# Feed-forward gate and up products: the high and low inputs as one 512-column moving operand, the halves added at eviction, and one set of accumulator banks in place of two

## What is computed

```
def swiglu(h, w_in, w_out):
    a, b = jnp.split(h @ w_in, 2, axis=-1)
    return (jax.nn.silu(a) * b) @ w_out
```

## Time and profile before

| | |
|---|---|
| Time before, median of 3 runs | 2448.12 us (2444.57 to 2448.9) |
| The profiled execution's own time | 2446.43 us |
| Its span | 2444.6 us, 35444 instructions |
| PE busy | 2278.1 us (93%), 15482 matmuls |
| PEld busy | 2061.0 us (84%) |
| DVE busy | 1291.6 us (53%) |
| ACT busy | 873.9 us (36%) |
| DMA | 373.10 MB, mean 153 GB/s |
| Mean granted clock of PE | 0.961 |

### The profile page before, as it was taken

One profiled execution on the slowest core, in us unless ns is written; L12 is line 12 of the kernel. 1 busy time (PEld: TensorE's weight loads), 2 busy tenths in 40 slices (PEclk: granted clock), 3 DMA queues, 4 the chain that ended last, 5 costly groups with the idle time before them and its releaser, 6 DMA issues.

```text
span 2444.6 us, 35444 instructions
## 1 busy us (share of the span) xinstructions
PE 2278.1 (93%) x15482; PEld 2061.0 (84%) x15482; DVE 1291.6 (53%) x1485; ACT 873.9 (36%) x889; POOL 123.3 (5%) x68
## 2 busy tenths in 40 slices
PE   6999889999999898999999899997999998889997
PEld 4887779999999568998998789987999886879996
DVE  4458535555653355546546545554555767535554
ACT  3313324335332143333334433333333442124332
POOL 0157200000000000000000000000000110000000
PEclk8999999999999999999999989998999996999998
DMA  7329604554554204555554315552455340024551
GB/s 305 115 101 390 290 1 179 183 184 172 180 183 170 77 2 154 184 182 184 189 187 157 121 69 189 182 183 99 176 185 189 123 171 1 1 71 157 182 184 52
DMA packets 52481, 373.10 MB, mean 153 GB/s; under 512 B 5728, under 2 KB 6752, under 8 KB 7840
## 3 DMA queue, kind: packets, MB, share of 16 engines
q1 hardware_dynamic: 51584, 367.78, 41.3%
q0 software_dynamic: 800, 3.93, 0.4%
HBM read 370.64 MB, written 1.05 MB: 152 GB/s over the span
## 4 chain that ended last, share of the span: by engine, by line
PE 89%; DVE 6%; ACT 3%; DMA 1%; issue 1%; POOL 0%; SPq 0%; DVEq 0%; ACTq 0%; POOLq 0%
PE PS L354 11%; PE PS L353 11%; PE PS L352 11%; PE PS L368 5%; PE PS L369 5%; PE PS L370 5%; PE PS L308 5%; PE PS L601 3%; PE PS L1267 2%; PE PS L753 2%; PE PS L290 2%; PE PS L291 2%; PE PS L192 2%; PE PS L292 2%; PE PS L273 2%; PE PS L274 2%
## 5 line engine op out<-in xcount | busy, mean ns | idle before, releaser
L473 DVE TENSOR_TENSOR ring_r<-ring,AR_r 128x2048 fp32r<-128x2048 f32 x274 | 628.3, 2298 | 584.9 <-ACT AR_r L467 584.9
L467 ACT ACTIVATE AR_r<-ring 128x2048 fp32r<-128x2048 f32 x274 | 522.2, 1911 | 584.2 <-PE PS L370 237.8
L352 PE MATMUL PS<-AR_r 128*128 128x256 f32 x2240 | 634.1, 283 | 0.0
L354 PE MATMUL PS<-AR_r,ring_r 128*128 128x256 f32 x2240 | 633.9, 283 | 0.0
L353 PE MATMUL PS<-AR_r 128*128 128x256 f32 x2240 | 633.9, 283 | 0.0
L353 PEld LDWEIGHTS PS<-AR_r 128*128 128x128 f32 x2240 | 429.8, 192 | 2.5
L352 PEld LDWEIGHTS PS<-AR_r 128*128 128x128 f32 x2240 | 429.8, 192 | 2.5
L354 PEld LDWEIGHTS PS<-AR_r,ring_r 128*128 128x128 f32 x2240 | 429.7, 192 | 0.0
L368 PE MATMUL PS<-AR_r 128*128 128x512 f32 x616 | 240.7, 391 | 0.0
L369 PE MATMUL PS<-ring_r,AR_r 128*128 128x512 f32 x616 | 240.5, 390 | 0.0
L370 PE MATMUL PS<-AR_r 128*128 128x512 f32 x616 | 239.6, 389 | 0.0
(11 more groups left out here) (362 smaller groups left out, 3146.8 us busy)
## 6 DMA issues: line engine op xcount, KB each, us to landing
ring<-stream SPq DMA_DIRECT2D x346, 1024.0 KB, 4.8
X<-xt SPq DMA_DIRECT2D x1, 2048.0 KB, 9.5
AR<-bias POOLq DMA_DIRECT2D x1, 1536.0 KB, 8.3
AR<-pt POOLq DMA_DIRECT2D x2, 512.0 KB, 4.2
out<-X SPq DMA_DIRECT2D x1, 1024.0 KB, 4.8
SM<-small SPq DMA_DIRECT2D x1, 545.0 KB, 4.0
AR<-invc SPq DMA_DIRECT2D x1, 512.0 KB, 15.1
X<-negl POOLq DMA_DIRECT2D x1, 512.0 KB, 7.5
```

The source lines that it names most:

```text
L352: pe.matmul(o, w_hi, X_HI[:, k, :], start=(k == 0), stop=False)
L354: ins = pe.matmul(o, w_lo, X_HI[:, k, :], start=False, stop=(k == DT - 1))
L467: act.activation(w_hi_of(tag, i), ring[:, n % SLOTS, :], ACT.Identity).then_inc(split_hi, 1)
L473: dve.tensor_tensor(RING_R[:, n % SLOTS, :], ring[:, n % SLOTS, :], w_hi_of(tag, i), ALU.subtract).then_inc(split_lo, 1)
```

## The change

`X_PARTS` is a view of the same memory as `X_HI` and `X_LO` with the two as its halves: for each `k` it gives 2 runs of 256 columns, 4096 elements apart. In `gate_up` one matmul of 512 columns with `w_hi` takes the place of the two of 256, and writes a whole bank: `w_hi*X_HI` into columns 0 to 255, `w_hi*X_LO` into columns 256 to 511. The matmul with `w_lo` adds to columns 0 to 255 as before. So each output tile `j` takes a bank of its own: the gate has banks 6 and 7 and the up product banks 4 and 5, in every step, where before steps went to two sets in turn. Step 0 is left as it was, in banks 4 and 5.

The two halves are added on the way out: ACT copies the low halves of both banks of the gate into `GATE` and of the up product into `HIDDEN` (`low_part`), DVE adds the high halves from the banks (new lines in `step` and `gating`), and silu and the products then work in place, outside the banks. A new semaphore `ffn_low` counts ACT's copies and `ffn_gate_taken` DVE's additions of the gate. PE waits for `ffn_gate_taken` of the step before ahead of a gate chunk, and for `ffn_gated` of the step before ahead of an up chunk.

```
@@ -141,6 +141,8 @@
         multiplied = S["chunk_multiplied"]
         ffn_silu = S["ffn_silu"]
         ffn_hidden = S["ffn_hidden"]
+        ffn_low = S["ffn_low"]
+        ffn_gate_taken = S["ffn_gate_taken"]
         ffn_gated = S["ffn_gated"]
         split_hi = S["split_hi"]
         split_lo = S["split_lo"]
@@ -172,6 +174,7 @@
         TURN_OF = {"ffn1_lat": 2, "ffn2": 2, "mix2_in": 2}
         w_hi_of = lambda tag, i: W0_HI[i % 3] if tag == "mix0_in" else W_HI[(i + TURN_OF.get(tag, 0)) % 3]
         X_HI, X_LO = (arena(at, DT, T, of=AR_R) for at in (12288, 16384))
+        X_PARTS = AR_R[:, 12288:20480].rearrange("p (s n) -> p s n", s=2)
         G_HI, G_LO = (arena(18432 + 1024 * i, 2, 2, T, of=AR_R) for i in range(2))
 
         def need_chunk(eng, n):
@@ -339,19 +342,22 @@
 
                 pe.wait_ge(split_lo, r + (s0 + i + 1))
 
-            def gate_up(d, i, r):
+            def gate_up(i, step, steps, r):
 
                 for half in range(2):
                     n = n0 + i + half
                     need_split(r, i + half)
+                    if half:
+                        pe.wait_ge(ffn_gated, steps + (g0 + step))
+                    elif c or step > 1:
+                        pe.wait_ge(ffn_gate_taken, steps + (c * (FF_STEPS - 1) + step - 1))
                     for j in range(2):
-                        o = PS[:, 4 + 2 * d + half, j * T:(j + 1) * T]
+                        bank = (6, 4)[half] + j
                         for k in range(DT):
                             w = slice(k * 256 + j * P, k * 256 + (j + 1) * P)
                             w_hi, w_lo = w_hi_of(tag, i + half)[:, w], RING_R[:, n % SLOTS, w]
-                            pe.matmul(o, w_hi, X_HI[:, k, :], start=(k == 0), stop=False)
-                            pe.matmul(o, w_hi, X_LO[:, k, :], start=False, stop=False)
-                            ins = pe.matmul(o, w_lo, X_HI[:, k, :], start=False, stop=(k == DT - 1))
+                            pe.matmul(PS[:, bank, :], w_hi, X_PARTS[:, :, k * T:(k + 1) * T], start=(k == 0), stop=False, skip_group_check=True)
+                            ins = pe.matmul(PS[:, bank, 0:T], w_lo, X_HI[:, k, :], start=False, stop=(k == DT - 1), skip_group_check=True)
                     ins.then_inc(multiplied, 1)
 
             def down(d, i, last, r):
@@ -384,12 +390,12 @@
             first = 0
             if sums:
                 turn()
-                gate_up(1, 2, 0)
+                gate_up(2, 1, 0, 0)
                 sums()
                 open_sums()
                 pe.wait_ge(ffn_gated, g0 + 1)
                 down(0, 4, False, 0)
-                gate_up(0, 5, 0)
+                gate_up(5, 2, 0, 0)
                 pe.wait_ge(ffn_gated, g0 + 2)
                 down(1, 7, False, 0)
                 first = 2
@@ -398,7 +404,7 @@
             with pe.Fori(0, (FF_STEPS - 1 - first) // 2) as r:
                 for it in (first + 1, first + 2):
 
-                    gate_up(it % 2, 3 * it - 1, r * 6)
+                    gate_up(3 * it - 1, it, r * 2, r * 6)
 
                     pe.wait_ge(ffn_gated, r * 2 + (g0 + it))
                     down((it - 1) % 2, 3 * it + 1, False, r * 6)
@@ -497,29 +503,46 @@
         def act_ffn(act, order, tag, between=None):
             n0 = START[tag]
 
-            def silu(it, r=0):
-
-                act.wait_ge(multiplied, r + (n0 + max(3 * it - 1, 0) + 1))
-                act.activation(GATE[:, it % 2, :], PS[:, 4 + 2 * (it % 2), :], ACT.Silu).then_inc(ffn_silu, 1)
-
-            def splits(it, r=0, turns=0):
-
-                for i in range(3 * it + (2 if it else 3), min(3 * it + 5, FF_CHUNKS)):
-                    act_split_chunk(act, tag, i, r, turns)
+            def silu(it, steps=0):
+
+                if it == 0:
+                    act.wait_ge(multiplied, n0 + 1)
+                    act.activation(GATE[:, 0, :], PS[:, 4, :], ACT.Silu).then_inc(ffn_silu, 1)
+                else:
+                    act.wait_ge(ffn_gate_taken, steps + (FFN_INDEX[tag] * (FF_STEPS - 1) + it))
+                    act.activation(GATE[:, it % 2, :], GATE[:, it % 2, :], ACT.Silu).then_inc(ffn_silu, 1)
+
+            def low_part(it, up, steps=0, r=0):
+                act.wait_ge(multiplied, r + (n0 + 3 * it + up))
+                if it >= 2:
+                    act.wait_ge(ffn_gated, steps + (FFN_INDEX[tag] * FF_STEPS + it - 1))
+                out, bank = (HIDDEN, 4) if up else (GATE, 6)
+                act.activation(out[:, it % 2, :].rearrange("p (j t) -> p j t", j=2), PS[:, bank:bank + 2, T:T2], ACT.Identity).then_inc(ffn_low, 1)
+
+            def splits(chunks, r=0, turns=0):
+
+                for i in chunks:
+                    if i < FF_CHUNKS:
+                        act_split_chunk(act, tag, i, r, turns)
+
+            def step(it, steps=0, r=0, turns=0):
+                low_part(it, 0, steps, r)
+                splits((3 * it + 2,), r, turns)
+                silu(it, steps)
+                low_part(it, 1, steps, r)
+                splits((3 * it + 3, 3 * it + 4), r, turns)
 
             act_table(act, order, ACT.Silu)
             silu(0)
-            splits(0)
+            splits((3, 4))
             if between:
                 between()
                 act_table(act, order, ACT.Silu)
             with act.Fori(0, (FF_STEPS - 3) // 2) as r:
                 for it in (1, 2):
-                    silu(it, r * 6)
-                    splits(it, r * 6, r)
+                    step(it, r * 2, r * 6, r)
             for it in (FF_STEPS - 2, FF_STEPS - 1):
-                silu(it)
-                splits(it)
+                step(it)
             act_ln_exp(act)
 
 
@@ -529,16 +552,22 @@
 
             def gating(it, steps=0, r=0):
                 d = it % 2
-                dve.wait_ge(ffn_silu, steps + (g0 + it + 1))
-
-                dve.wait_ge(multiplied, r + (n0 + (3 * it if it else 1) + 1))
+                gate, up = GATE[:, d, :], HIDDEN[:, d, :]
+                if it:
+                    dve.wait_ge(ffn_low, steps * 2 + (2 * FFN_INDEX[tag] * (FF_STEPS - 1) + 2 * it))
+                    halves_up = up.rearrange("p (j t) -> p j t", j=2)
+                    dve.tensor_tensor(halves_up, halves_up, PS[:, 4:6, 0:T], ALU.add).then_inc(ffn_hidden, 1)
+                else:
+                    dve.wait_ge(multiplied, n0 + 2)
+                    dve.tensor_copy(up, PS[:, 5, :]).then_inc(ffn_hidden, 1)
                 if it >= 2:
                     dve.wait_ge(multiplied, r + (n0 + 3 * it - 1))
-                gate, up = GATE[:, d, :], PS[:, 5 + 2 * d, :]
+                dve.wait_ge(ffn_silu, steps + (g0 + it + 1))
+                dve.wait_ge(ffn_hidden, steps * 3 + (3 * (g0 + it) + 1))
                 both = lambda ap: ap[:, d, :, :].rearrange("p a b -> p (a b)")
                 dve.tensor_tensor(both(G_HI), gate, up, ALU.mult).then_inc(ffn_hidden, 1)
-                dve.tensor_tensor(HIDDEN[:, d, :], gate, up, ALU.mult).then_inc(ffn_hidden, 1)
-                dve.wait_ge(ffn_hidden, steps * 2 + 2 * (g0 + it + 1))
+                dve.tensor_tensor(up, gate, up, ALU.mult).then_inc(ffn_hidden, 1)
+                dve.wait_ge(ffn_hidden, steps * 3 + 3 * (g0 + it + 1))
                 dve.tensor_tensor(both(G_LO), HIDDEN[:, d, :], both(G_HI), ALU.subtract).then_inc(ffn_gated, 1)
 
             gating(0)
@@ -548,6 +577,9 @@
                 add()
 
             def step(it, steps=0, r=0):
+                gate = GATE[:, it % 2, :].rearrange("p (j t) -> p j t", j=2)
+                dve.wait_ge(ffn_low, steps * 2 + (2 * FFN_INDEX[tag] * (FF_STEPS - 1) + 2 * it - 1))
+                dve.tensor_tensor(gate, gate, PS[:, 6:8, 0:T], ALU.add).then_inc(ffn_gate_taken, 1)
                 dve_split_chunk(dve, tag, 3 * it + 2, r)
                 gating(it, steps, r)
                 for i in range(3 * it + 3, min(3 * it + 5, FF_CHUNKS)):
```

## The result

The changed kernel takes 2433.41 us (median of 5 runs, 2430.32 to 2438.0) against 2448.3 us for the kernel before, run beside it. The ratio is 0.9944, with a 95% interval of 0.9930 to 0.9959: 13.7 us faster (10 to 17), where 2420, 28 us less, had been forecast. The sign was right and the time lies inside the range of 2405 to 2436; the gain is half of the 26.7 us that the sum gave.

The account below looks back on a forecast made before the run. The prediction took PE's matmul stream to bound the blocks. A pair at 347.8 ns for a triple at 359.7 saved 11.9 ns, times 2240 is 26.7 us; waits and eviction cost nothing, giving 2420 us, range 2405 to 2436.

Parts of the forecast that it names:

- the sum: Whole kernel: 11.9 ns saved per pair times 2240 is 26.7 us, ends 29.6 and 17.5, giving 2420 us.
- What bounds the kernel: Inside the feed-forward blocks PE's stream sets the time; DVE and ACT, the evicting engines, have room.
- One matmul less is worth 13.2 ns: Gate and up chunks: each matmul costs about 13 ns beyond its columns at either width; one in three goes.
- the price of the pair: Gate and up chunks: 227.9 ns, a down chunk's mean, plus 119.9 is 347.8 ns, against 359.7 for the triple.
- first rival: Gate and up chunks: 512-column matmuls stay at 232 ns, each following one of 256; 2429 us, chance 0.2.
- down chunks unchanged: Down chunks, 24 matmuls of 512 columns: they would still take 5.47 us each.
- the same 232 ns behind a rise of the clock: Argument against the 232 ns rival: six such gaps (44.17 to 45.56 us) without change of width, perhaps unrelated settling.
- slower: Gate and up chunks: each change from 256 to 512 pays 27 ns; +30.9 us, 2477 us, chance 0.09.
- The operand in two runs at no cost: Merged matmul's moving operand: the jump between its two runs costs nothing; a second start would cost 13.2 ns.
- Both waits at nothing: PE ahead of gate and up chunks: waits of 1.3 and 3.4 us are covered by 11.0 us of other work.
- The tight place: First two blocks, gate splits of steps 2 and 3: margins of 0.3 and 1.5 us, costed at nothing.
- The range: Forecast time of the whole kernel: 2405 to 2436 us, with about 2 in 10 left out.

Follow-up runs that it names:

- three-narrow kernel: Changed kernel with only the merging undone, three matmuls of 256 columns again, new eviction and waits kept; 2447.57 us, ratio 1.0017.
- Both-wide: Changed kernel with the second matmul of each pair widened to 512 columns, adding a fourth product; 2654.36 us, ratio 1.0863.
- narrow-grouped: Changed kernel without merged matmuls, per chunk first all 32 of 256 columns with high weights, then 16 with low ones; 2447.61 us, ratio 1.0006.
- grouped kernel: Changed kernel with the same matmuls reordered, per chunk first the 16 of 512 columns, then the 16 of 256; 2416.03 us, ratio 0.9882.
- one-run kernel: Changed kernel with a contiguous moving operand of 512 columns in place of two runs, so it computes something else; 2433.95 us, ratio 0.9958.
- twos: Changed kernel with two matmuls of 512 columns, then two of 256, in turn; 2420.38 us, ratio 0.9890.

## Why the prediction had the gain twice too large

**What bounds the kernel** was right: PE's stream sets the time in the blocks, before and after, and DVE and ACT took the new work into their idle time. The three-narrow kernel shows it by itself.

**One matmul less is worth 13.2 ns** was right for streams of one width. Both-wide has 226.7 ns, narrow-grouped 120.0, and the grouped kernel gets 28.7 us from 2240 fewer matmuls, near the 29.6 that the sum's upper end gave. The matmul's excess is its own. The 2.5 ns that the Trainium skill ("TensorE: Matmul & The Clock Gate", "Back-to-back issue gap") gives for an isolated matmul doesn't fit any of these streams: by it 512 columns would take an estimated 215.8 ns, and they took 226.7.

**The step that failed** is the price of the pair, 227.9 + 119.9 = 347.8 ns: it measured 352.8. The mean over a down chunk spreads one change of width over 24 matmuls, and in the changed kernel every matmul of 512 stands behind one of another width. The nearest row was that of the first five gaps, 232 ns, which gives 351.9. That is the first rival, which had 0.2 and a time of 2429. Its sum was right to 1 ns, but partly by luck: once the alternation is under way the gaps are 236.0 and 116.8 ns in the mean, so the wide matmul's excess is larger than it had and the narrow one is cheaper.

A second term was put at nothing, "down chunks unchanged": they took 5.50 us and not 5.47. Together they are the shortfall: 2240 x 5.0 ns is 11.2 us and the down chunks are 2.1, together 13.3 us, where 13.0 of the 26.7 were missing.

What spoke against the first rival, the same 232 ns behind a rise of the clock, didn't exclude that a change of width does it too. The row of 256 and 128 columns in turn did tell against the large charge of 27 ns for each change, and rightly. But that rival, called slower, had the mechanism that the runs showed, a cost of the change of width; it was wrong in the size, 27 ns where 6 were measured, and so in the sign of the whole.

**The operand in two runs at no cost** was right, by the one-run kernel. **Both waits at nothing** was right: PE has no wait there, and the three-narrow kernel has the same sum of gaps as the kernel before. **The tight place** was right in its sizes: the margin at step 3 was forecast at 1.5 us and is 1.8. The range held the time, but its middle came from the wrong row.

What stays open is the mechanism behind the change of width. Shown is that it goes with the widths and not with runs, weights' place, banks or order, that it is 6 ns a pair with 256, 320 or 384 columns beside 512 in alternation, and 1.6 with twos of 256. The width of a matmul is that of its moving operand and of what it writes; no run tells these two apart. Nor is it shown for every pair of widths: the turns of 256 and 128 columns had nothing over the earlier trace rows. The repeat over three pairs in the changed kernel isn't explained.

## What to carry to other kernels

Price a matmul in a mixed stream by the rows directly behind a change, not by a mean over a long run of one width. When matmuls are merged to wider ones, keep the narrow rest in a group of its own: here that doubled the gain, from a ratio of 0.9944 to 0.9882, with the same instructions. Even groups of two get nearly all of it (0.9890).

## What the runs showed of the hardware that I had not expected

Matmuls of fp32r at full clock cost their columns and about 13 ns more each (120.0, 226.7 ns at 256 and 512 columns). At 512 columns the next weights can hardly be what they wait for: the row of their load, 188 ns long, starts 3 ns behind the matmul and ends ahead of the next. A matmul beside one of another width departs from that: alternating with 256, 512 columns take 232 to 240 ns, and 256 columns between two of 512 take 113 to 120, so a short one can be cheaper in a mixed stream than among its own kind. The wide one loses more than the short one gains, and it takes some five matmuls behind a long run of 256 (before), some ten behind the alternation (after), to settle at 226.7. So the charge of a change isn't fixed: it is about 6 ns for each change from 256 to 512 in the alternation, 3 in twos (1.6 a pair), and 28 on the first five wide ones behind a group of 16 narrow ones in the grouped kernel's up chunk (233.7, 235.6, 228.6, 232.3, 231.0), less 7 that the first two narrow ones had saved. Groups of 16 still win, because there are so few changes.
